# A hybrid decoder step on one core: four key buffers in decode attention, seven-product output projections, late pages on GpSimd's queue, scaled keys on ScalarE

## The reference

```
hid = einsum(blocks of 32 rows, w1) -> silu -> w2          # compress: keys and values, past pages included
p = masked_softmax(q k^T + bias(distance)); o = p v        # three times, gated, summed
s = s * g_last + swapaxes(k_dec) @ u                       # delta-rule state, per sequence
```

## Time and profile before

| | |
|---|---|
| runs | 2648.28 us median of 3 (2647.49 to 2650.5) |
| profiled execution | 2645.75 us, its span 2644.1 us, mean granted clock 0.956 |
| TensorE | 2383.5 us busy (90%) |
| weight loads | 1780.8 us (67%) |
| VectorE | 1056.3 us (40%) |
| ScalarE | 532.8 us (20%) |
| GpSimd | 948.2 us (36%) |

### The profile page before, as it was taken

The page is one execution under the profiler, slowest core; times in us unless marked ns, Lnnn a source line. Parts: engine busy times, 40 slices in busy tenths (PEclk is TensorE's granted clock), DMA queues, the critical chain, the costliest instruction groups (busy, mean ns, idle before and its releaser), DMA issues. The chain is left out here.

```text
span 2644.1 us, 38267 instructions
## 1 busy us (share of the span) xinstructions
PE 2383.5 (90%) x15378; PEld 1780.8 (67%) x15378; DVE 1056.3 (40%) x1957; ACT 532.8 (20%) x1161; POOL 948.2 (36%) x832
## 2 busy tenths in 40 slices
PE   6997799669999999999996998989998999999997
PEld 4775444336777777766774767777775767777775
DVE  2001777322541132167886545364442034402412
ACT  1001566221000000135552212132320010000000
POOL 1320355101763355375653121222112036544640
PEclk9998899879999999999997999999998999999998
DMA  6622100351111221221115020020202112122210
GB/s 244 212 86 87 32 1 1 128 196 64 64 64 64 96 80 48 98 91 64 64 64 56 6 96 3 22 81 21 81 6 100 64 65 78 51 93 80 80 64 36
DMA packets 51735, 193.69 MB, mean 73 GB/s; under 512 B 15650, under 2 KB 26658, under 8 KB 35314
## 3 DMA queue, kind: packets, MB, share of 16 engines
q1 hardware_dynamic: 45922, 175.76, 19.7%
q0 software_dynamic: 3344, 14.56, 1.7%
q10 hardware_dynamic: 2304, 1.05, 0.1%
HBM read 170.79 MB, written 28.81 MB: 75 GB/s over the span
## 5 line engine op out<-in xcount | busy, mean ns | idle before, releaser
L217 PE MATMUL ps<-xn,ring 128*128 128x288 f32 x896 | 222.8, 413 | 9.5 <-DVEq L242 6.7
L1525 PE MATMUL ps<-hid,ring 128*128 128x288 f32 x768 | 194.8, 410 | 23.0 <-DVE hid L1621 23.0
L217 PEld LDWEIGHTS ps<-xn,ring 128*128 128x128 f32 x896 | 173.3, 194 | 58.4 <-issue 6.9
L1525 PE MATMUL ps<-xn,ring 128*128 128x288 f32 x768 | 202.2, 412 | 9.2 <-DVE xn L1605 8.7
L1566 POOL TENSOR_TENSOR wsum<-ring 128x512 f32<-128x512 f32 x64 | 81.8, 1279 | 323.6 <-POOLq L111 131.4
L1525 PEld LDWEIGHTS ps<-hid,ring 128*128 128x128 f32 x768 | 146.4, 191 | 64.7 <-DVE hid L1621 24.8
L1525 PEld LDWEIGHTS ps<-xn,ring 128*128 128x128 f32 x768 | 146.4, 192 | 54.1 <-issue 8.2
L1589 POOL TENSOR_TENSOR prod<-prod,rstd 128x1152 f32<-128x1152 f32 x32 | 83.7, 2617 | 180.7 <-DVE prod L1667 163.5
L1551 ACT ACTIVATE p<-ps 128x288 f32<-128x288 f32 x48 | 19.7, 410 | 631.5 <-PE ps L1525 631.5
L2604 PE MATMUL ps<-xn,ring 128*128 128x288 f32 x512 | 138.3, 416 | 3.0 <-PE ps L2668 1.7
L1525 PE MATMUL ps<-x_sum,wsum 128*128 128x288 f32 x512 | 134.5, 417 | 3.2 <-DVE x_sum L1608 2.5
(11 more groups left out here) (403 smaller groups left out, 4575.0 us busy)
## 6 DMA issues: line engine op xcount, KB each, us to landing
ring<-in_w_mlp SPq DMA_DIRECT2D x64, 1024.0 KB, 4.9
ring<-in_w_gdn_in SPq DMA_DIRECT2D x16, 1024.0 KB, 4.9
ring<-in_w_nsa_in SPq DMA_DIRECT2D x10, 1024.0 KB, 8.7
ring<-in_w_gdn_z SPq DMA_DIRECT2D x8, 1024.0 KB, 4.9
x<-in_seq_state SPq DMA_DIRECT2D x4, 2048.0 KB, 8.4
out_seq_state<-x SPq DMA_DIRECT2D x4, 2048.0 KB, 11.2
ring<-in_w_gdn_out SPq DMA_DIRECT2D x8, 1024.0 KB, 5.8
out_win_old<-in_win_rows POOLq DMA_DIRECT2D x1, 8064.0 KB, 47.6
```

Source lines behind the costliest of these rows:

```text
L217: mm = nc.tensor.matmul(S.pairs[:, pair, half, :], w, x[:, half * HT:half * HT + HT], start=first, stop=last)
L1525: mm = nc.tensor.matmul(S.ps[:, base + BANK[p], 0:HT], stationary(p, blk.units[pair // 4], pair % 4), moving(blk.kind, p, pair), start=pai ...
```

## The change

- Decode attention: a fourth buffer (the space of `S.toep`), in turn `n % 4`. Window keys and rows are issued by GpSimd's queue (`kv_load_window`), pages by SP's (`kv_load_pages`), each with semaphores of its own, and `qk(w)` waits only for what its branch reads. GpSimd issues sequences 1 to 3 before the first new-key scores, and 4 to 7 at even w, behind a wait for `pv`. TensorE's step is now `turn(w-2)`, `times_v(w-3)`, `qk(w)`. The residual and the units of the projection are loaded earlier (after sequences 4, 5, 6).
- The late pages of ScalarE's queue are issued by GpSimd's.
- Both output projections get the seven-product form (`add_seven_stage`), four blocks of 7 x 4 and of 7 x 8 products, with block 0 in the order 1, 2, 5, 6, 7, 4, 3. In the second the residual's return is issued inside the new stage and no longer in `gdn_stage`. Weights are laid out in quarters on the host.
- `scaled_keys` is now four ScalarE activations with a factor for each row, behind the norm's output and before `tile_end`.
- `by_sequence` spreads over 4 columns by a mask for sequence mod 4 (512 columns), and product h reads rows 32h to 32h+31.

```diff
-            late_pages(act, 1)
+            pool.wait_ge(product, 2)
+            late_pages(pool, 1)
...
+def kv_load_window(eng, S, n):
+    win_keys, win_rows, _ = kv_view(S, n % KV_BUFFERS)
+    landed = S.kv_window_in[n % KV_BUFFERS] if n else S.kv_first_in
+    eng.dma_start(win_keys, S.dram["win_keys"][n]).then_inc(landed, 16)
+    eng.dma_start(win_rows, S.dram["win_rows"][n, :, 256:512].rearrange("(j p) c -> p j c", p=128)).then_inc(landed, 16)
...
         @block.sync
             for n in range(1, NSEQ):
-                before = [m for m in range(n) if KV_BUFFER[m] == KV_BUFFER[n]]
-                if before:
-                    sp.wait_ge(pv, last[before[-1]] + 1)
-                kv_load(sp, S, n)
-            sp.wait_ge(pv, last[5] + 1)
-            for u in (0, 1):
-                sp.dma_start(S.ring[:, u], out_d.weights[u]).then_inc(out_d.loaded[u], 16)
-            sp.wait_ge(pv, last[6] + 1)
+                if n >= KV_BUFFERS:
+                    sp.wait_ge(pv, last[n - KV_BUFFERS] + 1)
+                kv_load_pages(sp, S, n)
+            sp.wait_ge(pv, last[4] + 1)
             sp.dma_start(S.x[:].rearrange("p k t -> p (k t)"), S.x_dram[:]).then_inc(x_back, 16)
-            sp.wait_ge(pv, last[7] + 1)
-            for u in (2, 3):
-                sp.dma_start(S.ring[:, u], out_d.weights[u]).then_inc(out_d.loaded[u], 16)
+            for n, slots in ((5, (2, 3)), (6, (0, 1))):
+                sp.wait_ge(pv, last[n] + 1)
+                for u in slots:
+                    sp.dma_start(S.ring[:, u], out_d.weights[u]).then_inc(out_d.loaded[u], 16)
...
         @block.gpsimd
+            for n in range(1, KV_BUFFERS):
+                kv_load_window(pool, S, n)
+            pool.wait_ge(news_set, 2)
             for w in range(3):
                 new_scores(w)
...
             for w in range(3, NW):
                 new_scores(w)
+                n = w // 2 + 2
+                if w % 2 == 0 and KV_BUFFERS <= n < NSEQ:
+                    pool.wait_ge(pv, last[n - KV_BUFFERS] + 1)
+                    kv_load_window(pool, S, n)
...
             for w in range(2, NW + 5):
-                if w < NW:
-                    qk(w)
                 if w - 2 < NW:
                     turn(w - 2)
                 if 0 <= w - 3 < NW:
                     times_v(w - 3)
+                if w < NW:
+                    qk(w)
...
+def add_seven_stage(S, name, pairs, q, nxt, room=None, back=None):
...
+        order = lambda n: PRODUCTS if n else (1, 2, 5, 6, 7, 4, 3)
...
+        @block.sync
+            if back is not None:
+                sp.wait_ge(*back)
+                sp.dma_start(S.x[:].rearrange("p k t -> p (k t)"), S.x_dram[:]).then_inc(x_back, 16)
...
+        @block.tensor
+            for n, units in enumerate(blocks):
...
+                for p in order(n):
...
+                    if p == 2:
+                        pe.wait_ge(p1_read, n + 1)
+                    elif p == 7:
+                        pe.wait_ge(u2_set, n + 1)
+                    elif p == 3:
+                        pe.wait_ge(c22, n + 1)
+                    if p in W_SUMMED:
+                        pe.wait_ge(w_summed, per * (4 * n + W_SUMMED[p]))
+                    if n == 0 and p in SUMMED:
+                        pe.wait_ge(summed, SUMMED[p])
+                    for pair in range(pairs):
+                        mm = nc.tensor.matmul(S.ps[:, base + BANK[p], 0:HT], stationary(p, units[pair // 4], pair % 4),
+                                              moving(p, pair), start=pair == 0 and p in OPENS, stop=pair == pairs - 1,
+                                              skip_group_check=True)
...
+        @block.vector
+            v.tensor_tensor(by_pair[0], q[:, :, :, 1], q[:, :, :, 0], ALU.subtract).then_inc(summed, 1)
...
+            if back is not None:
+                dve.wait_ge(x_back, 16)
+            for n in range(4):
+                after(5)
+                v.tensor_tensor(x22, x22, c, ALU.add).then_inc(c22, 1)
+                after(6)
+                v.tensor_tensor(u2[:, n % 2], p1[:, n % 2], b, ALU.add).then_inc(u2_set, 1)
...
-            sp.wait_ge(seq_out, 64)
-            sp.dma_start(S.x[:].rearrange("p k t -> p (k t)"), S.x_dram[:]).then_inc(S.x_back, 16)
...
-                        mm = nc.tensor.matmul(S.ps[:, 2 * h, :], B["kdec"][0:TS, j, :],
-                                              ue[j % 2][:, 4 * h:4 * h + 4, :].rearrange("p n v -> p (n v)"), start=True, stop=True)
+                        r = slice(32 * h, 32 * h + 32)
+                        mm = nc.tensor.matmul(S.ps[:, 2 * h, :], B["kdec"][r, j, :],
+                                              ue[j % 2][r].rearrange("p n v -> p (n v)"), start=True, stop=True)
...
+                for j in range(4):
+                    k = a_.activation(buf[b][name][0:rows, j, :], S.ps[0:rows, 4 * b + 3, 256 + 128 * (j // 2):384 + 128 * (j // 2)],
+                                      ACT.Copy, scale=factor[0:rows, i, 4 * hg + j:4 * hg + j + 1])
+                done(k, c, "act")
...
-                    if n < 2:
-                        scaled_keys(c, b, i, job, hg, *(("kb", S.upto), ("kdec", S.rest))[n], pr)
...
-                    v.tensor_tensor(ue[j % 2], B["u"][0:TS, j:j + 1, :].broadcast_to([TS, NSEQ, 128]),
-                                    S.c("seq_of")[0:TS, :].unsqueeze(2).broadcast_to([TS, NSEQ, 128]), ALU.mult).then_inc(ue_set, 1)
+                    v.tensor_tensor(ue[j % 2], B["u"][0:TS, j:j + 1, :].broadcast_to([TS, 4, 128]),
+                                    S.c("seq_in_half")[0:TS, :].unsqueeze(2).broadcast_to([TS, 4, 128]), ALU.mult).then_inc(ue_set, 1)
...
-    add_to_residual(S, S.dense["gdn_out"], lambda k: S.gq[:, 8 * (k // 4) + 4 + k % 4], nxt=S.dense["mlp1"], ready=(S.x_back, 16))
+    q = S.gq[:].rearrange("p (g e m) (h t) -> p g e (m h) t", g=4, m=2, h=2)[:, :, 2:4]
+    add_seven_stage(S, "gdn_out", 8, q, S.dense["mlp1"],
+                    back=S.seq_stored, room=S.xn[:].rearrange("p (s a) (h t) -> p s (a h) t", s=2, h=2))
```

More of the change, by code:

```diff
@@ L419, in nsa_in_stage @@
     early = [sem(f"cmp_pages{u}_in") for u in range(3)]
-    late = [sem(f"cmp_pages3_{q}") for q in ("sp", "act")]
+    late = [sem(f"cmp_pages3_{q}") for q in ("sp", "pool")]
     prompt_in, product, bias_set = sem("cmp_prompt_in"), sem("cmp_product"), sem("cmp_bias_set")
@@ L679, in prompt_attention_stage @@
         cpv, o_done, o_out = sem("pa_cpv"), sem("pa_o_done"), sem("pa_o_out")
-        S.kv_in = [sem(f"da_kv_in{b}") for b in range(3)]
+        S.kv_in = [sem(f"da_kv_in{b}") for b in range(KV_BUFFERS)]
+        S.kv_window_in, S.kv_first_in = [sem(f"da_kv_window_in{b}") for b in range(KV_BUFFERS)], sem("da_kv_first_in")
         block = ctx.enter_context(nc.Block())
@@ L1001, in kv_view @@
 def kv_view(S, buffer):
-    tile = S.x[:].rearrange("p k t -> p (k t)")[:, 0:4096] if buffer == 0 else (
-        S.ring[:, 4 - 2 * buffer:6 - 2 * buffer].rearrange("p s c -> p (s c)"))
+    tile = (S.x[:].rearrange("p k t -> p (k t)")[:, 0:4096], S.ring[:, 2:4].rearrange("p s c -> p (s c)"),
+            S.ring[:, 0:2].rearrange("p s c -> p (s c)"), S.toep[:].rearrange("p h d -> p (h d)"))[buffer]
     win_keys = tile[:, 0:1024].rearrange("p (k t) -> p k t", k=2)
@@ L1008, in kv_view, with kv_load_pages @@
     return win_keys, win_rows, pages
[L1011 to L1024, removed]
+KV_BUFFERS = 4
+def kv_load_window(eng, S, n):
[3 more added lines that the diff above has]
+    eng.dma_start(win_rows, S.dram["win_rows"][n, :, 256:512].rearrange("(j p) c -> p j c", p=128)).then_inc(landed, 16)
+def kv_load_pages(sp, S, n):
+    _, _, pages = kv_view(S, n % KV_BUFFERS)
+    landed = S.kv_in[n % KV_BUFFERS]
     for j in range(NPG):
@@ L2288, in gdn_stage @@
         zm = sb("gdn_zm", [128, NSEQ, 128])
-        ue = [tiles[0:TS, 1, at:at + 2].rearrange("p n j v -> p (n j) v")
-              for at in (names.index("vb"), names.index("qk"))]
+        ue = [buf[1][k][0:TS] for k in ("vb", "qk")]
         C = [Counted(S, f"gdn_tile{p}", tile_steps(LEVELS)) for p in range(2)]
@@ L2704, in tile_front, with scaled_keys @@
                 yield
+            def scaled_keys(c, b, i, job, hg, pr, name, factor):
+                rows = rows_of(c)
+                wait_step(act, c, "pe", job, "turned")
+                if name == "kb":
+                    for n, _, nb, nj in norms_before(hg, pr):
+                        if nb == b:
+                            wait_step(act, n, "pe", nj, "out_turned")
+                else:
+                    wait_step(act, c, "vec", job, "it")
+                    if pr == 0:
+                        wait_step(act, Q, "pe", hg)
+                for j in range(4):
+                    k = a_.activation(buf[b][name][0:rows, j, :], S.ps[0:rows, 4 * b + 3, 256 + 128 * (j // 2):384 + 128 * (j // 2)],
+                                      ACT.Copy, scale=factor[0:rows, i, 4 * hg + j:4 * hg + j + 1])
```

(1 more changed line is left out.)

189 lines of the change are left out of this document (145 added, 44 removed).

## The result

The changed kernel takes 2564.98 us, the median of 4 runs (2558.23 to 2569.93), beside 2648.12 us for the kernel before (2647.49 to 2650.5, 4 runs). The ratio is 0.9683, 95% interval 0.9656 to 0.9709: 83 us less. The forecast was 2547 with a range of 2534 to 2574. The profiled execution took 2558.23 us (span 2555.6, granted clock 0.963) and is the fastest of the four; its counterpart before took 2645.75.

What follows compares the result with a forecast made beforehand. TensorE, busy in 90% of the span, was taken as the bound, with idle gaps in three places. Six terms sum to -101.2 us: 2645.75 profiled becomes 2544.6, plus 2.5 for the median gives 2547 us, range 2534 to 2574.

Steps and rivals of the forecast that it cites:

- Term 1: NSA input stage: late pages on GpSimd's queue free ScalarE's first SiLU, -15.0 us (bounds -16.5 and -9).
- Term 2: Decode attention: value products ahead of the wait, four buffers, loads on two queues, -40 us (bounds -24 and -46).
- decode attention ... in 72 us: Sign of success: decode attention from its first transpose to the projection in 72 us, loads of two sequences in flight.
- Rival (b): Decode attention: loads stay the bound, a sequence costs 9.9 us, only -24 us there, total 2563; chance 18%.
- rival (e): NSA input stage: late pages miss by 6 us, total 2553; chance counted within the forecast's 60%.
- Terms 4 and 5: Delta rule: scaled keys on ScalarE, -11.5 us (0 to -12); state products with 32 rows side by side, -13.6 us.
- Rivals (a) and (c): Delta rule: (a) 32-row products run one behind the other, 2561, 15%; (c) ScalarE's keys late or slowing merges, 2558, 5%.
- Term 3: Output projection of NSA: 128 products become 4 blocks of 28, -6.7 us (-8 to -4).
- Term 6: Output projection of the delta rule: 256 products become 224, stage starts 1.6 us earlier, -14.4 us (-17 to -9).
- Rival (d): Decode attention: GpSimd's queue delivers windows so slowly that decode grows, total about 2660; chance 2%.

Runs made afterwards that it cites:

- the best version: Changed kernel plus scores first, third row-sum buffer, second sequence's window on SP, ring buffers exchanged, kv output behind late pages, gates' round trip before it: 2541.50 us.

## Why the prediction was right, and where its terms were not

The time lies in the range, 18 us above the forecast. 13.7 of these are between the forecast (2544.6) and the profiled execution (2558.23); the other 4.3 are that the runs' median stands 6.7 above the profiled execution, the fastest of four, and not 2.5. Part of the agreement is luck: terms 1 and 2 together fell 14.5 us short, and the 3.0 us of the first MLP, which no term forecast, made up for some of it. Of the signs, "decode attention ... in 72 us" failed at 81.4.

- **Term 2, decode attention, +9.8 of the 13.7.** Its account of before was right: with three buffers the value products ahead of the wait take most of the load waits away, and with four all but the first. It failed at the next limit, "with the transposes right behind the next window's softmax I take 2.65": in the changed kernel a sequence takes 6.7 to 6.9 us and not 5.3, and the first 9.1. I had moved the value products ahead and asked only what they no longer wait for. I had not asked what the score product, now last in the step, does to those who wait for it. The stage with scores first has 5.16 us a sequence, 2.58 a window, and the best version's 67.57 is below my 71.6: the data side of the forecast (loads at up to 6.3 us a sequence) holds, the products' side too, and only the chain between engines was missing. The start (5.83 us of wait for the window where I had charged 3 us of extra time) is the smaller part. The wait that I did name and put at nothing, GpSimd's for a value product ahead of its loads ("I count nothing"), is 0.35 us here, and 2.73 once scores come first. Rival (b), the load as the bound, is not what happened. Its remark that every restart after a stall is at half clock holds for the five load waits of 5.3 to 8.5 us in the loop before (1.93 us for eight records) and not for the one of 2.71 us (1.06, at 484.40).
- **Term 1, late pages, +4.7.** The gap of 15.07 went, and GpSimd's issue pace was as forecast (last issue at 234.01 for 233). What failed is "The output of kv and the gate rows on SP now run into the stage's end; they take about 1": this transfer of 3.4 MB runs beside the last pages and makes one of them land 7.5 us after its issue. With the output behind the pages and the gates' round trip ahead of it, the compression takes 48.89 us where the kernel before took 65.81, so -16.9 was there to be had. It is near rival (e) in size, with another cause: not a slow pace of issue but a transfer that had been behind the pages' use and now starts beside them.
- **Terms 4 and 5** came out at 11.54 and 13.62 for 11.5 and 13.6, each in its place, when undone alone. Rivals (a) and (c) fall. For the pair of products the Trainium skill ("TensorEngine Tiling (Array Packing)", Restrictions and Gotchas) would allow the overlap in banks 0 and 2, and the 1.13 us agree; no run wrote one bank.
- **Term 3** was 5.5 for 6.7. The stage starts at half clock for 8.4 us in this execution (until 555.4), in the kernel before for 5.7. That costs half of the difference, an estimate of 1.4 us from these two stretches, about what is missing. In six of the experiments the stage took 60.3 to 60.9 us, which would be 7.3 to 7.9; in the other five 62.7 to 63.3. No run undid the seven products of either projection, so terms 3 and 6 rest on the table alone.
- **Term 6** was 15.3 for 14.4: 13.8, and the 1.5 that terms 4 and 5 leave of the delta rule's 26.7, a remainder that no run tested. VectorE's four sums take 13.3 us and not 20, so the wait for its read of product 6 is 0.55 and not 2.5.
- Rival (d), GpSimd's queue so slow that decode grows, needed 173 us of decode attention; it takes 81.4.

## What to carry to other kernels

When an instruction is moved ahead of a wait, follow also the one that moved back: who stands behind it on the other engines, and through which buffer of two they are tied to one another. Once a resource is doubled, try the old order again; here the fourth buffer made the new order unnecessary, and it cost more than it gave. Before an engine with compute work gets loads to issue, list what stands behind each load's wait in its own list. When an engine's queue is cleared, list the large transfers that will now start earlier, and put them behind the small ones that someone waits for.

## What the runs showed of the hardware

- The same instructions of prompt attention take 206.6 to 206.8 us in five profiled executions and 209.6 to 211.8 in eight. Window rows of one turn of its loop, first of the changed kernel, then of the one with keys on VectorE: 23.43 us at full clock, 23.90 at 0.93, with one stretch at half clock in each turn from there on; the changed kernel has such stretches only in two turns near the stage's end. In the rows shown TensorE idles 2.1 us of the turn at full clock and 1.3 of the other. Why the clock falls in one execution and not in another was not tried; that it also makes the runs of one kernel differ by 10 us is only argued from this.

```profile
335.40:358.83 23.43, 21.31 (x132) 10.81 (x133) 18.24 (x54) 15.16 (x48) 11.53 (x13) 1.00 0.00 1
```

```profile
335.40:359.30 23.90, 22.57 (x133) 11.59 (x133) 18.28 (x54) 15.15 (x47) 11.55 (x12) 0.93 0.00 1
```

- A late page of 64 KB lands 1.7 to 2.2 us after its issue when the 3.4 MB output stands behind all pages, and up to 7.5 us when this output is issued 0.4 us before the last of them.
- VectorE's sum of 2304 columns took 2.56 to 3.62 us beside GpSimd's sums, where 1152 columns took 2.45 in the earlier trace rows: the time did not double with the columns. GpSimd's sums gave way too: in the first output projection one of 512 columns took 2.26 to 2.38 us beside them and 1.27 once they were over (557.61).
